# First feed-forward: the operand's low halves ahead of the second weight unit's remainder, and the first activation table loaded at the start

## The chip, the cores and the metric

The kernel runs on one core of one Trainium2 chip. The metric is the device time of one execution in microseconds (us); less is better. For the kernel before there are three timed runs, and one execution taken by the hardware profiler.

## The reference

Two transformer blocks, one behind the other, on 512 tokens of width 1024, all in float32. Only the first step of the first block matters here:

```python
def rms_norm(x, g):
    xf = x.astype(jnp.float32)
    y = xf * lax.rsqrt(jnp.mean(xf * xf, axis=-1, keepdims=True) + EPS)
    return (y * g.astype(jnp.float32)).astype(x.dtype)

def swiglu(h, w_gate, w_up, w_down):
    return (jax.nn.silu(h @ w_gate) * (h @ w_up)) @ w_down

x = x + 0.5 * swiglu(rms_norm(x, g_ffn1), w1_gate, w1_up, w1_down)   # D_FF = 2816
...
```

Behind it come a mixer with sparse and stick-breaking attention, a second feed-forward, a second mixer (mLSTM and differential attention) and a mixture of experts.

## The kernel before

**Products in three parts.** Each float32 product is made of three matmuls on a faster type. An operand is split into a high half (a rounded copy, made by ScalarE) and a low half (what the rounding left out, made by VectorE by subtraction). `mm3` (line 1178) issues high x high, high x low and low x high, for every k of the eight slices of the width. A slice is 128 x 512.

**The operand.** x lies transposed in `xT`, eight slices of 128 x 512. `operand` on ScalarE (line 1674) writes the high half `hH` of slice k, times the gain g_ffn1; `operand` on VectorE (line 2152) writes the low half `hL`. The factor of the norm is applied later: `square` on ScalarE (line 1678) squares a slice, `square` on VectorE (line 2156) adds it to `acc`, one matmul with a matrix of ones sums over the partitions, and `norm` on ScalarE (line 1664) takes the logarithm and the exponential of it. The products with w1_gate and w1_up are multiplied by that factor once they are done.

**Weight units.** Weights come in units of 128 x 1024 (512 KB), here the 128 columns of one output tile for all eight k. A ring of five landing tiles (`stage`) takes the transfers, and a ring of four (`wH`) the high halves. `round_weights` on ScalarE (line 1646) makes the high half of a unit, `remainder` on VectorE (line 2126) the low half, in place of the landed data. Unit 0 is the first tile of w1_gate, unit 1 the first of w1_up, unit 2 the second of w1_gate, and so on in turn. `weights_to(n)` on either engine handles all units up to n that have not been handled. In the steady state the engines handle unit i + 2 when TensorE is about to begin unit i (`AHEAD` is 2).

**Order.** Every engine has its own program and works it off in order; semaphores tie the programs together. TensorE's `dense` (line 1198) waits for the remainder of its unit (`w_lo`), and in the first unit also, ahead of each k, for the low half of the operand (`h`). So TensorE needs from VectorE: remainder 0 and low half 0, then low halves 1 to 7 one by one, then remainder 1, then the complete sum of squares for the norm's matmul, then remainder 2. The opening of the ScalarE program is at lines 2103 to 2111, that of the VectorE program at lines 2744 to 2751. VectorE's order is low half 0, remainder 0, low halves 1 and 2, remainder 1, low halves 3 to 7, squares. ScalarE's is high half 0, unit 0, high halves 1 to 7, squares 0 and 1, unit 1, squares 2 to 7.

**Transfers.** SyncE's program (line 2854 on) issues the gains (`cols`), then x in four pieces of two slices, with unit 0 behind the first piece, then unit 1, the constant matrices, units 2 and 3, more matrices, and from then on one unit whenever a landing tile is free.

**Activation tables.** ScalarE holds one set of functions at a time. `table(name)` (line 1637) remembers the set last asked for and issues a load when another is wanted; Copy and Square are in every set used here. Where an activation comes ahead of any load, the build puts one in front of it by itself. `norm` asks for "log_exp", the step `gate_r` behind it for "silu".

Of the kernel before, what the change touches and what calls it, by code (L numbers as in the profile page):

```python
# [20 lines left out]
NSTAGE, NSPLIT, AHEAD = 5, 4, 2  # L21
# [110 lines left out]
class Counts:  # L132
# [24 lines left out]
    def after(self, stream, *key):  # L157
        if not self.real:
            return None, 1
        name, n = self.at[(stream,) + key]  # L160
        return self.sem(name), n
# [73 lines left out]
def build(nc, A, out):  # L235
    with contextlib.ExitStack() as ctx:
# [1397 lines left out]
        def act_program(act):  # L1634
# [11 lines left out]
            def round_weights(u):  # L1646
                act.wait_ge(*after("land%d" % u.raw.at, u.i))
                free(u.high)
                act.activation(u.high.t[:, 0:u.size], u.raw.t[0][:, 0:u.size], ACT.Copy).then_inc(*did("w_hi", u.i))

            def weights_to(n):
                while state["unit"] <= min(n, M3.main - 1):
                    if not units[state["unit"]].whole:
                        round_weights(units[state["unit"]])
                    state["unit"] += 1
# [18 lines left out]
            def operand(s):  # L1674
                act.wait_ge(*after(*s.ready))
                act.activation(h[0][:, s.k, :], xT[:, s.k, :], ACT.Copy, scale=col(s.gain, s.k)).then_inc(*did("hh", s.gain, s.k))

            def square(s):
                act.wait_ge(*after(*s.ready))
                if s.k == 0:  # L1680
                    act.activation(acc[:, :], xT[:, 0, :], ACT.Square).then_inc(*did("acc0", s.gain))
                else:
                    if s.k > 2:
                        act.wait_ge(*after("acc", s.gain, s.k - 2))
                    act.activation(xsq[s.k % 2][:, :], xT[:, s.k, :], ACT.Square).then_inc(*did("sq", s.gain, s.k))
# [368 lines left out]
            def moe_stage(steps, M):  # L2054
# [35 lines left out]
                def region(x):  # L2090
                    seen = dict(act.passed)
                    state["table"] = None
                    counts.engine = "scalar_done_extra"
                    with act.when(count, x):
                        expert_steps(M.regions[x])
                        if x == 0:
                            for more in range(1, NX):
                                region(more)
                    act.passed, counts.engine = seen, "scalar_done"

                region(0)

            act.wait_ge(*after("cols_in",))
            for k in range(8):
                operand(Step("operand", gain="g_ffn1", k=k, ready=("x_in%d" % (k // 2),)))
                if k == 0:
                    weights_to(0)
            for k in range(8):
                square(Step("square", gain="g_ffn1", k=k, ready=("x_in%d" % (k // 2),)))
                if k == 1:  # L2110
                    weights_to(AHEAD - 1)
            ffn_stage(ffn1)
            mixer1_stage(mix1, M1)
            ffn_stage(ffn2)
# [4 lines left out]
        def dve_program(dve):  # L2119
# [6 lines left out]
            def remainder(u):  # L2126
                dve.wait_ge(*after("w_hi", u.i))
                dve.tensor_tensor(u.raw.t[1][:, 0:u.size], u.raw.t[0][:, 0:u.size], u.high.t[:, 0:u.size].bitcast(F32), ALU.subtract).then_inc(*did("w_lo", u.i))

            def weights_to(n):  # L2130
                while state["unit"] <= min(n, M3.main - 1):
                    if not units[state["unit"]].whole:
                        remainder(units[state["unit"]])
                    state["unit"] += 1
# [17 lines left out]
            def operand(s):  # L2152
                dve.wait_ge(*after("hh", s.gain, s.k))
                dve.scalar_tensor_tensor(h[1][:, s.k, :], xT[:, s.k, :], col(s.gain, s.k), h[0][:, s.k, :].bitcast(F32), ALU.mult, ALU.subtract).then_inc(*did("h", s.gain, s.k))
# [589 lines left out]
            for k in range(8):  # L2744
                operand(Step("operand", gain="g_ffn1", k=k))
                if k == 0:
                    weights_to(0)
                if k == 2:
                    weights_to(AHEAD - 1)
            for k in range(8):  # L2750
                square(Step("square", gain="g_ffn1", k=k))
            ffn_stage(ffn1)
# [160 lines left out]
        for program, done in ((sp_program, "sync_done"), (pe_program, "matmul_done"), (act_program, "scalar_done"),  # L2913
                              (dve_program, "vector_done"), (pool_program, "gpsimd_done")):
            run(program, Lane(None), done)
        counts.real = True
        counts.n = {}
        with nc.Block() as block:
            @block.sync
            def _(e):  # L2920
                run(sp_program, Lane(e), "sync_done")

            @block.tensor
            def _(e):
                run(pe_program, Lane(e), "matmul_done")

            @block.scalar
            def _(e):
                run(act_program, Lane(e), "scalar_done")

            @block.vector
            def _(e):
                run(dve_program, Lane(e), "vector_done")

            @block.gpsimd
            def _(e):
                run(pool_program, Lane(e), "gpsimd_done")
# [57 lines left out]
```

## Time and profile before

| | us |
|---|---|
| median of three runs | 2161.86 |
| the three runs | 2161.70, 2161.86, 2169.89 |
| time of the profiled execution | 2164.77 |
| its span | 2163.0 |
| TensorE busy (matmul) | 2065.1 (95% of the span) |
| VectorE busy | 1356.5 (63%) |
| ScalarE busy | 1019.1 (47%) |
| mean granted TensorE clock | 0.965 of full |

Times in the trace are counted from the start of the span; the execution's own time is 1.8 us longer than its span. Matmul ends are modelled, so the distance between starts is the safer measure of pace.

### The profile page before, as it was taken

To read this page: it belongs to the slowest core of one execution; us is meant where nothing else is said; L and a number is where in the kernel's file an instruction comes from. 1 tells how busy PE (TensorE), PEld (TensorE's weight loads), DVE (VectorE), ACT (ScalarE), POOL (GpSimd) and SP (SyncE) were. 2 spreads that over 40 slices of the span, in tenths; PEclk is the share of its full clock that TensorE was granted. 3 is DMA by queue.
4 is the path that set the end of the run, shared out by engine and by line. 5 is a ranking of instruction groups with operands and counts; after the bars stand their busy time and mean duration, and the time that the engine had idled before them with its cause. 6 is when DMAs were issued, how large, how long until landed. Compare 5 with 4: busy or idle time off the path is not lost.

```text
span 2163.0 us, 23488 instructions
## 1 busy us (share of the span) xinstructions
PE 2065.1 (95%) x9192; PEld 1575.6 (73%) x9192; DVE 1356.5 (63%) x1900; ACT 1019.1 (47%) x1504; POOL 125.7 (6%) x115
## 2 busy tenths in 40 slices
PE   7999999979999889999999999998979999999998
PEld 6888887746787668888888787775766666666664
DVE  5443544466666876544344465556788888888886
ACT  5222323344444354422122344555567777667773
POOL 0000000000000000000000000000012112111110
PEclk9999999988898899999999999999989999999999
DMA  5433334336334214333333332220549999999996
GB/s 179 146 99 110 90 96 80 85 48 65 55 61 67 73 40 146 96 96 91 101 96 97 88 101 58 56 59 25 184 173 397 394 391 392 391 386 384 390 386 231
DMA packets 289719, 351.68 MB, mean 163 GB/s; under 512 B 14768, under 2 KB 228784, under 8 KB 289600
## 3 DMA queue, kind: packets, MB, share of 16 engines
q1 hardware_dynamic: 280080, 326.43, 47.4%
q0 software_dynamic: 9520, 23.66, 3.1%
q8 instruction: 75, 1.23, 0.2%
q14 instruction: 44, 0.36, 0.0%
HBM read 337.71 MB, written 20.45 MB: 166 GB/s over the span
## 4 chain that ended last, share of the span: by engine, by line
PE 82%; DVE 10%; ACT 5%; DMA 1%; issue 1%; SPq 0%; DVEq 0%; ACTq 0%
PE bank L181 81%; PE bank L184 2%; ACT p L187 1%; DMA stage<-w_in 1%; ACT wH L187 1%; DVE PTL L193 1%; DVE y L193 1%; DVE score L217 1%; ACT T L187 1%; ACT rr L187 1%; DVE st L205 1%; DVE p L196 1%; DVE top L214 1%; DVE stage2L L193 0%; DVE gt L193 0%
## 5 line engine op out<-in xcount | busy, mean ns | idle before, releaser
L181 PE MATMUL bank<-hH,wH 128*128 128x512 f32 x1104 | 445.8, 404 | 14.4 <-DVE stage0L L193 9.9
L181 PE MATMUL bank<-hL,wH 128*128 128x512 f32 x1104 | 438.1, 397 | 0.0
L187 ACT ACTIVATE wH<-stage 128x1024 fp32r<-128x1024 f32 (+3 forms) x265 | 262.4, 1002 | 98.8 <-PE bank L181 81.4
L181 PEld LDWEIGHTS bank<-hH,wH 128*128 128x128 f32 x1104 | 213.7, 194 | 65.8 <-DVE stage0L L193 9.9
L181 PEld LDWEIGHTS bank<-hL,wH 128*128 128x128 f32 x1104 | 213.6, 193 | 45.1 <-issue 1.2
L187 ACT ACTIVATE w_moe<-stage_moe 128x1024 fp32r<-128x1024 f32 x158 | 156.8, 1047 | 0.2 <-issue 0.2
L181 PE MATMUL bank<-w_moe,xS 128*128 128x512 f32 x382 | 154.0, 403 | 0.0
L181 PE MATMUL bank<-hidH,wH 128*128 128x512 f32 x352 | 137.4, 390 | 2.1 <-DVE stage2L L193 0.9
L181 PE MATMUL bank<-hidL,wH 128*128 128x512 f32 x352 | 136.9, 389 | 0.0
L187 ACT ACTIVATE hidH<-hf 128x512 fp32r<-128x512 f32 x44 | 27.8, 632 | 189.1 <-DVE hf L193 189.1
L199 DVE SCALAR_TENSOR_TENSOR xT<-bank,xT 128x512 f32<-128x512 f32 x32 | 22.1, 692 | 133.6 <-PE bank L181 133.6
L187 ACT ACTIVATE sg<-sg 128x512 f32<-128x512 f32 x60 | 36.9, 628 | 124.5 <-DVE sg L193 124.5
L181 PEld LDWEIGHTS bank<-w_moe,xS 128*128 128x128 f32 x382 | 71.8, 188 | 30.9 <-issue 16.2
L193 DVE TENSOR_TENSOR stage1L<-stage,wH 128x1024 fp32r<-128x1024 f32 (+2 forms) x56 | 67.1, 1199 | 40.1 <-ACT wH L187 39.8
L181 PE MATMUL bank<-hH,stage3L 128*128 128x512 f32 x232 | 91.7, 395 | 0.0
L181 PE MATMUL bank<-hH,stage1L 128*128 128x512 f32 x224 | 88.4, 395 | 0.0
L181 PE MATMUL bank<-stage_moe,hF 128*64 128x512 f32 x192 | 87.5, 598 | 0.0
L181 PE MATMUL bank<-hH,stage2L 128*128 128x512 f32 x216 | 86.0, 398 | 0.0
L181 PE MATMUL bank<-hH,stage4L 128*128 128x512 f32 x216 | 85.5, 396 | 0.0
L193 DVE TENSOR_TENSOR stage0L<-stage,wH 128x1024 fp32r<-128x1024 f32 (+3 forms) x56 | 63.7, 1137 | 34.2 <-ACT wH L187 33.7
L187 ACT ACTIVATE hH<-xT,cols 128x512 fp32r<-128x512 f32 x40 | 28.3, 721 | 119.7 <-DVE xT L199 83.8
L181 PE MATMUL bank<-hH,stage0L 128*128 128x512 f32 x208 | 83.1, 400 | 0.0
(576 smaller groups left out, 4565.9 us busy)
## 6 DMA issues: line engine op xcount, KB each, us to landing
stage<-w_up SPq DMA_DIRECT2D x88, 512.0 KB, 5.8
stage_moe<-w_gate SPq DMA_DIRECT2D x88, 512.0 KB, 6.3
stage_moe<-w_down SPq DMA_DIRECT2D x88, 512.0 KB, 7.4
stage<-w_gate SPq DMA_DIRECT2D x84, 512.0 KB, 5.5
stage_moe<-w_up SPq DMA_DIRECT2D x84, 512.0 KB, 7.8
stage<-w_in SPq DMA_DIRECT2D x58, 512.0 KB, 4.4
stage<-w_down SPq DMA_DIRECT2D x56, 512.0 KB, 6.7
pair_results<-zero POOLq DMA_DIRECT2D x8, 512.0 KB, 2.9
```

What stands on the lines that cost most here:

```text
L181: return self.e.matmul(*a, **k) if self.e is not None else Nothing()
L184: return self.e.transpose(*a, **k) if self.e is not None else Nothing()
L187: return self.e.activation(*a, **k) if self.e is not None else Nothing()
L193: return self.e.tensor_tensor(*a, **k) if self.e is not None else Nothing()
L196: return self.e.tensor_scalar(*a, **k) if self.e is not None else Nothing()
L199: return self.e.scalar_tensor_tensor(*a, **k) if self.e is not None else Nothing()
L205: return self.e.tensor_reduce(*a, **k) if self.e is not None else Nothing()
L214: return self.e.max(*a, **k) if self.e is not None else Nothing()
L217: return self.e.match_replace(*a, **k) if self.e is not None else Nothing()
```

## The change

The ScalarE program asks for the silu set ahead of its first wait. Both programs then work through all eight slices of the operand before they turn to unit 1 (`AHEAD - 1` is 1), and take the squares behind that. TensorE's, GpSimd's and SyncE's programs are as they were.

```diff
@@ -2100,15 +2100,15 @@
 
                 region(0)
 
+            table("silu")
             act.wait_ge(*after("cols_in",))
             for k in range(8):
                 operand(Step("operand", gain="g_ffn1", k=k, ready=("x_in%d" % (k // 2),)))
                 if k == 0:
                     weights_to(0)
+            weights_to(AHEAD - 1)
             for k in range(8):
                 square(Step("square", gain="g_ffn1", k=k, ready=("x_in%d" % (k // 2),)))
-                if k == 1:
-                    weights_to(AHEAD - 1)
             ffn_stage(ffn1)
             mixer1_stage(mix1, M1)
             ffn_stage(ffn2)
@@ -2745,8 +2745,7 @@
                 operand(Step("operand", gain="g_ffn1", k=k))
                 if k == 0:
                     weights_to(0)
-                if k == 2:
-                    weights_to(AHEAD - 1)
+            weights_to(AHEAD - 1)
             for k in range(8):
                 square(Step("square", gain="g_ffn1", k=k))
             ffn_stage(ffn1)
```

## Rows read from the trace of the kernel before

**Rows 1.** The page, part 4: shares of the chain that ended last, by engine.

```profile
PE 82%; DVE 10%; ACT 5%; DMA 1%; issue 1%; SPq 0%; DVEq 0%; ACTq 0%
```

**Rows 2.** That chain in order of time, 0 to 80 us: start, duration, what.

```profile
5.61 1.28 ACT L187
...
16.82 63.21 PE bank L181 x269
```

**Rows 3.** Timeline, TensorE, 9 to 30 us: start, duration, instruction [idle before, releaser].

```profile
9.89 0.80 PE L181 MATMUL bank<-hH,wH 128*128 128x512 f32 x1 [9.89 <-DVE stage0L L193]
10.48 0.63 PE L181 MATMUL bank<-hL,wH 128*128 128x512 f32 x1
...
13.04 0.45 PE L181 MATMUL bank<-hL,wH 128*128 128x512 f32 x1
13.33 0.40 PE L181 MATMUL bank<-hH,stage0L 128*128 128x512 f32 x1
16.82 0.79 PE L181 MATMUL bank<-hH,wH 128*128 128x512 f32 x1 [3.10 <-DVE hL L199]
...
21.84 0.40 PE L181 MATMUL bank<-hH,wH 128*128 128x512 f32 x1
...
27.29 1.02 PE L181 MATMUL bank<-acc,mats 128*128 128x512 f32 x2
27.75 0.79 PE L181 MATMUL bank<-hH,wH 128*128 128x512 f32 x1
```

**Rows 4.** Timeline, ScalarE (two rows), then VectorE, 0 to 40 us.

```profile
8.48 4.38 ACT L187 ACTIVATE hH<-xT,cols 128x512 fp32r<-128x512 f32 x7
...
23.78 1.99 ACT L187 ACTIVATE wH<-stage 128x1024 fp32r<-128x1024 f32 x2
...
7.66 0.75 DVE L199 SCALAR_TENSOR_TENSOR hL<-xT,cols,hH 128x512 fp32r<-128x512 f32 x1 [7.66 <-ACT hH L187]
...
9.75 1.41 DVE L199 SCALAR_TENSOR_TENSOR hL<-xT,cols,hH 128x512 fp32r<-128x512 f32 x2
14.88 1.23 DVE L193 TENSOR_TENSOR stage1L<-stage,wH 128x1024 fp32r<-128x1024 f32 x1 [3.73 <-ACT wH L187]
16.02 3.40 DVE L199 SCALAR_TENSOR_TENSOR hL<-xT,cols,hH 128x512 fp32r<-128x512 f32 x5
19.34 5.47 DVE L193 TENSOR_TENSOR acc<-acc,xsq 128x512 f32<-128x512 f32 x7
```

**Rows 5.** Four issues of SyncE; under each its KB and us from issue to landing.

```profile
1.67 0.43 SPq L223 DMA_DIRECT2D stage<-w_gate  x1
stage<-w_gate SPq DMA_DIRECT2D x1, 512.0 KB, 5.5
...
3.24 0.52 SPq L223 DMA_DIRECT2D xT<-x  x1
xT<-x SPq DMA_DIRECT2D x1, 512.0 KB, 7.9
...
3.80 0.45 SPq L223 DMA_DIRECT2D stage<-w_up  x1
stage<-w_up SPq DMA_DIRECT2D x1, 512.0 KB, 9.1
...
7.37 3.89 SPq L223 DMA_DIRECT2D stage<-w_up  x1
stage<-w_up SPq DMA_DIRECT2D x1, 512.0 KB, 10.0
```

**Rows 6.** Busy time by stretch, single engines, then granted clock, DMA share, GB/s.

```profile
16.60:20.00 3.40, 3.17 (x8) 2.50 (x9) 3.40 (x6) 0.00 (x0) 0.00 (x0) 0.50 0.82 239
400.00:760.00 360.00, 326.24 (x1470) 254.52 (x1470) 235.43 (x448) 159.93 (x280) 8.67 (x16) 0.88 0.38 64
```

**Rows 7.** Groups of instructions, the table loads: count, busy, mean ns, idle before.

```profile
L190 ACT ACT_TABLE_LOAD x14 | 18.0, 1283 | 27.7 <-PE bank L181 19.4 <-DVE so L193 5.6 <-DVE sg L193 1.6
L187 ACT ACT_TABLE_LOAD x1 | 1.3, 1283 | 5.6 <-DMA xT<-x 5.6
```

## Prediction

> **What bounds the kernel now.** I read the chain that ended last first, as shares and then in order of time over the first 80 us; then the TensorE timeline of the opening, then ScalarE and VectorE beside it, then the landing times of the first transfers. The chain is 82% TensorE [rows 1], and from 16.82 us on it is TensorE without a gap for far longer than the 80 us asked for [rows 2]. So the body of the kernel is a line of matmuls, and time taken out ahead of 16.82 us moves everything behind it. Before that the chain holds a table load of 1.28 us at 5.61 [rows 2], ScalarE's high halves and the remainder of the second weight unit at 14.88 [rows 4].
>
> The TensorE timeline shows what that costs. The first matmul starts at 9.89, behind the remainder of unit 0. Nine matmuls (three of the eight k) run, and then the engine stands for 3.10 us until 16.82, waiting for a VectorE low half [rows 3]. The cause is in the order of VectorE's work. Low halves 1 and 2 are done at 11.16; then VectorE sits 3.73 us idle for the rounded high half of unit 1, makes its remainder from 14.88, and only at 16.02 begins low halves 3 to 7, which TensorE needs first [rows 4]. ScalarE had all eight high halves ready at 12.86 (8.48 + 4.38) [rows 4]. The stall is a matter of order, not of capacity.
>
> It costs a second time. At the start matmuls 2 to 8 are 0.427 apart ((13.04 - 10.48)/6), and the step from 8 to 9 is 0.29: the pace has just risen. In unit 1 it is 0.227 ((27.29 - 21.84)/24). But behind the stall the other fifteen matmuls of unit 0 take 5.02, from 16.82 to 21.84, where 15 x 0.227 would be 3.41 [rows 3]: the granted clock is at 0.50 from 16.6 to 20.0, the lower level of 1.2 GHz [rows 6].
>
> **The change, part by part.** I rebuild the opening with the durations and start-to-start distances of the rows.
>
> *The table load.* Before, it runs at 5.61, behind the wait for x, and the first high half, at 6.9, follows its end (5.61 + 1.28) [rows 2]. After, it is issued ahead of every wait, with some 4.8 us of idle ScalarE as its cover (0.8 to 5.6) against its 1.28. No other load is added: the trace has fourteen loads by the helper and one automatic one [rows 7], and Copy and Square both run while the silu set is in, so the automatic one should go. If the cover were gone, the cost would be what it is today. The first high half then starts at about 5.6 and ends near 6.3. But next on ScalarE is the rounding of unit 0, and that transfer was issued at 1.67 and landed 5.5 later, at 7.17 [rows 5]. So rounding starts at about 7.24 and not at 7.54 (where it would follow today's high half): of 1.28 us only 0.30 arrives. The rest is idle ScalarE waiting for weights. First matmul: 9.89 - 0.30 = 9.59. Bounds: 0 (if the landing slips by 0.3) and 1.28 (if it came early).
>
> *The order on VectorE.* With the start 0.30 earlier, low half 1 begins at 9.45. The five in a row take (3.40 - 0.75)/4 = 0.66 each, start to start, where 0.75 is one alone [rows 4], so low half 7 begins at 9.45 + 6 x 0.66 = 13.4 and is done at 14.2. ScalarE supplies ahead of it: seven high halves take 4.38 from about 8.18, so to 12.56; the last pair of x lands at 3.24 + 7.9 = 11.1 [rows 5], before high half 6 would start (11.25). That margin is 0.1 us, and even if it is lost VectorE does not want high half 6 until 12.7.
>
> *TensorE.* Matmul 1 at 9.59, matmul 2 0.59 later [rows 3], then 0.427 each while the clock is low. In the profiled execution the pace changed at about 13.2, between matmuls 8 and 9. If it does so at the same time, matmul 9 starts near 13.17, matmul 10 near 13.45, and the remaining ones follow at 0.227: matmul 24 at 13.45 + 14 x 0.227 = 16.63, and unit 1 at 16.86. k = 3 is wanted at 13.4 and has been there since 11.5; k = 7 is wanted at about 16.0 and is there at 14.2. No low half is late.
>
> *What is late next: the remainder of unit 1.* Its weights were issued at 3.80 and landed 9.1 later, at 12.90 [rows 5]. ScalarE, free at 12.56, rounds them from 12.97 to 14.01; VectorE takes the remainder at 14.1, done at 15.3. TensorE wants it at 16.86: 1.6 us to spare. So the wait that is moved behind the low halves does not hold TensorE. Queued behind it on VectorE are only the sums of squares.
>
> *Sums of squares, and units 2 and 3.* Rounding unit 1 now comes ahead of the squares on ScalarE, but VectorE's seven additions set the pace. They start right after the remainder, at 15.23 and not 19.34, and take 5.47 [rows 4]: done at 20.7. TensorE reaches the norm matmul after 24 matmuls, which took 27.29 - 21.84 = 5.45 before, hence at 22.31; unit 2 begins 0.46 behind that, as before at 27.75 [rows 3]. Spare: 1.6. The remainder of unit 2 follows from 20.75 to 21.98, wanted at 22.77: spare 0.8, the smallest margin in the new opening. Both roundings before it start at 19.7 instead of 23.78 [rows 4]; the data of unit 3, issued at 7.37, is there at 17.4 [rows 5]. The transfers that follow wait for TensorE's completions and move with it.
>
> *Sum.* Unit 1 starts at 16.86 instead of 21.84 [rows 3]: 4.98, call it 5.0. It has three parts: 3.26 is the stall (13.33 to 16.82, less one 0.23); 1.61 is the second slow stretch (5.02 against 3.41); 0.30 is the table, of which about half is lost again, since the start falls in the slow pace. Everything later waits on something earlier, not on a fixed time, so the shift is carried to the end. Span 2163.0 - 5.0 = 2158.0; the profiled execution's own time 2164.8 - 5.0 = 2159.8. The median of the three runs was 2161.9, 2.9 below that execution, so my figure for the median is 2161.9 - 5.0 = **2156.9**.
>
> **The rivals.**
>
> *A: the low clock lasts longer in the new opening (12%).* What speaks for it: no row says what would fix the moment of the rise, and in this trace the low stretch behind the stall lasted 3.4 us [rows 6]. If the slow pace lasted that much longer in the new opening, 8 matmuls would run in place of 15, and 7 x 0.227 = 1.6 us go. The gain is 3.4: median 2158.5. Against: the engine is busier than before from its first matmul on. On the pages: the Trainium skill ("TensorE: Matmul & The Clock Gate", Part 1: The HAM clock gate) says that the gate's count runs free of the kernel, so that the moment of the rise varies from run to run; the trace has one execution only and can neither bear that out nor refute it.
>
> *B: the table's full 1.28 us arrives (4%).* That needs the first weights about 1 us earlier than in the trace. Nothing in the change moves a transfer. It would add 0.5 (in the slow pace half of an earlier start is lost) to 1.0: gain about 5.7, median 2156.2.
>
> *C: the gain is absorbed or the table part is void (8%).* Should the automatic load stay, 0.30 is lost: 2157.2. Should unit 2's remainder come more than 0.8 us late (ScalarE and VectorE alternate on squares in steps of 0.8, so one lost step uses the margin), TensorE pauses at 22.8 and perhaps 1 to 3 us return: 2158 to 2160.
>
> *D: the clock of the first mixer (6% to the slow side of before, 4% to the fast side).* From 400 to 760 us the granted clock averages 0.88 [rows 6], so (1 - 0.88) x 2 x 360 = 86 us lie at the low level. A matmul costs 0.427 there against 0.227, so a further 3.4 us at that level costs up to 3.4 x 0.47 = 1.6. The new opening shifts the mixer against whatever sets these stretches. From four more low stretches on the gain is gone (4 x 1.6 = 6.4: median 2163); for 0.5% slower it takes ten more. For it: the three runs of the same kernel spread by 8 us. Against: it can as well go the other way (the 4%, which adds 6 us or more to the gain), and most such stretches come from the stage's own waits, which the change does not touch.
>
> **How the numbers follow.** Forecast 66% (2156.9, give or take 1.5), A 12%, B 4%, C 8%, D 6% slow and 4% fast. The range takes in A to C (2156 to 2160) and the spread that the runs of one kernel show, in either direction: D's first step above, the same mechanism in our favour below. 2151 to 2164. A measurement of this kernel tells a change from none at about 0.5%, which is 10.8 us. The forecast and A, B and C lie within it. Only D reaches beyond: all its 4% on the fast side, where the gain of 5.0 adds to it, and 2 of its 6% on the slow side.
>
> **What would show it.** The first ScalarE row is a load by the helper's line, before 3 us. High half 0 starts at 5.6, the rounding of unit 0 at 7.2, now with an idle that a transfer ends. First matmul at 9.6. VectorE: seven low halves in a row from about 9.45, remainder of unit 1 at 14.1. TensorE: no idle between matmul 9 and 10, unit 1 from 16.9, norm matmul near 22.3. Table switch behind the norm at 23.3, not 28.3. I would be wrong if TensorE shows a new wait at 16.9 (unit 1's remainder) or at 22.8 (unit 2's), if the clock falls inside the opening all the same, or if the shift of 5.0 at 28 us has shrunk by the end of the feed-forward.

## The result and the profile after

| | before | after |
|---|---|---|
| median, us | 2167.01 (22 runs, 2161.48 to 2170.30) | 2161.68 (22 runs, 2155.32 to 2165.81) |
| time of the profiled execution | 2164.77 | 2162.40 |
| its span | 2163.0 | 2160.6 |
| first matmul of unit 0 / of unit 1 / norm matmul, at us | 9.89 / 21.84 / 27.29 | 9.47 / 17.48 / 22.92 |

The change is faster: ratio 0.9978, 95% interval 0.9971 to 0.9985, which is 5.3 us between the medians. The kernel before was run again beside it, and its median over 22 runs is 2167.01. The three runs shown earlier had given 2161.86, close to the lowest of the 22. Beside the experiments below the same kernel gave medians of 2165.21, 2165.19 and 2166.04 (33, 33 and 23 runs).

The TensorE timeline of the changed kernel, to be laid beside [rows 3]; columns are start, duration, instruction, and in brackets the idle before it:

```profile
9.47 0.79 PE L181 MATMUL bank<-hH,wH 128*128 128x512 f32 x1 [9.47 <-DVE stage0L L193]
10.06 0.63 PE L181 MATMUL bank<-hL,wH 128*128 128x512 f32 x1
...
13.05 0.63 PE L181 MATMUL bank<-hH,stage0L 128*128 128x512 f32 x1
13.47 0.63 PE L181 MATMUL bank<-hH,wH 128*128 128x512 f32 x1
...
14.33 0.60 PE L181 MATMUL bank<-hH,stage0L 128*128 128x512 f32 x1
14.76 0.40 PE L181 MATMUL bank<-hH,wH 128*128 128x512 f32 x1
14.99 0.39 PE L181 MATMUL bank<-hL,wH 128*128 128x512 f32 x1
...
17.48 0.39 PE L181 MATMUL bank<-hH,wH 128*128 128x512 f32 x1
...
22.92 1.02 PE L181 MATMUL bank<-acc,mats 128*128 128x512 f32 x2
23.38 0.79 PE L181 MATMUL bank<-hH,wH 128*128 128x512 f32 x1
```

Only the first row has an idle. k = 3 follows k = 2 at once (13.47 behind 13.05), where [rows 3] has 3.10 us. But the slow pace, 0.43 from start to start, lasts twelve matmuls, up to 14.76, and not the eight of [rows 3].

ScalarE (first six rows) and VectorE in the same execution, beside [rows 4]:

```profile
0.75 1.28 ACT L190 ACT_TABLE_LOAD   x1 [0.75 <-PEq L2987]
5.43 0.72 ACT L187 ACTIVATE hH<-xT,cols 128x512 fp32r<-128x512 f32 x1 [3.40 <-DMA xT<-x]
7.10 1.06 ACT L187 ACTIVATE wH<-stage 128x1024 fp32r<-128x1024 f32 x1 [0.95 <-DMA stage<-w_gate]
8.06 4.38 ACT L187 ACTIVATE hH<-xT,cols 128x512 fp32r<-128x512 f32 x7
12.77 1.06 ACT L187 ACTIVATE wH<-stage 128x1024 fp32r<-128x1024 f32 x1 [0.33 <-DMA stage<-w_up]
...
23.97 1.28 ACT L190 ACT_TABLE_LOAD   x1 [2.42 <-PE bank L181]
...
9.33 4.72 DVE L199 SCALAR_TENSOR_TENSOR hL<-xT,cols,hH 128x512 fp32r<-128x512 f32 x7
13.97 1.22 DVE L193 TENSOR_TENSOR stage1L<-stage,wH 128x1024 fp32r<-128x1024 f32 x1
15.10 5.47 DVE L193 TENSOR_TENSOR acc<-acc,xsq 128x512 f32<-128x512 f32 x7
20.63 1.23 DVE L193 TENSOR_TENSOR stage2L<-stage,wH 128x1024 fp32r<-128x1024 f32 x1
```

The load is over at 2.03, and the next row is 3.40 us of waiting for x. The one behind it shows why the load's 1.28 us don't arrive: ScalarE then stands 0.95 us for the transfer of w_gate. VectorE works without a gap from 9.33 on, and unit 1's remainder is done at 15.19, 2.3 us before TensorE begins unit 1.

The chain that ended last, in order of time (start, duration, what), says the same in one view, beside [rows 2]. The table and all of the operand's high halves have left it, and a weight transfer stands in their place:

```profile
1.67 5.41 DMA stage<-w_gate
7.08 0.02 issue
7.10 1.06 ACT wH L187
8.16 0.02 issue
8.19 1.24 DVE stage0L L193
9.43 0.04 issue
9.47 70.73 PE bank L181 x298
```

The groups of table loads, beside [rows 7]: fifteen by the helper, and no automatic one is left.

```profile
L190 ACT ACT_TABLE_LOAD x15 | 19.2, 1283 | 28.2 <-PE bank L181 19.2 <-DVE so L193 5.6 <-DVE sg L193 1.6
```

### The profile page after: what moved, and what is told of

Read it like the earlier page. It is cut to its first block, busy times and chain, and to the rows that moved or that the text cites. A ratio compares the mean times of both kernels' runs of the same rounds, so it can differ in the third digit from the quotient of the medians.

```text
span 2160.6 us, 23488 instructions
## 1 busy us (share of the span) xinstructions
PE 2067.6 (96%) x9192; PEld 1576.3 (73%) x9192; DVE 1356.9 (63%) x1900; ACT 1019.5 (47%) x1504; POOL 126.7 (6%) x115
## 4 chain that ended last, share of the span: by engine, by line
PE 83%; DVE 10%; ACT 5%; DMA 1%; issue 1%; SPq 0%; DVEq 0%; ACTq 0%
PE bank L181 81%; PE bank L184 2%; ACT p L187 1%; DMA stage<-w_in 1%; DVE PTL L193 1%; ACT wH L187 1%; DVE y L193 1%; DVE score L217 1%; ACT T L187 1%; ACT rr L187 1%; DVE st L205 1%; DVE p L196 1%; DVE top L214 1%; DVE stage2L L193 0%; DVE gt L193 0%
```

## The experiments

Ratios are to the kernel before, run on the same chip in the same turns, with 95% intervals. "Unit 1" is the start of its first matmul in the profiled execution; "pace rises" is the first matmul that starts less than 0.3 us behind the one before it.

| kernel | ratio | first matmul | pace rises | unit 1 |
|---|---|---|---|---|
| before | 1 | 9.89 | 13.33 (and again 20.2) | 21.84 |
| the change | 0.9978 (0.9971 to 0.9985) | 9.47 | 14.99 | 17.48 |
| order only | 0.9980 (0.9971 to 0.9989) | 9.78 | 15.34 | 17.88 |
| table only | 1.0004 (0.9995 to 1.0014) | 9.55 | 21.74 | 22.43 |
| VectorE's order only | 0.9981 (0.9972 to 0.9991) | 10.23 | 13.59 | 17.23 |
| ScalarE's order only | 0.9993 (0.9983 to 1.0002) | 9.71 | 16.44 | 19.42 |
| stall filled | 0.9993 (0.9982 to 1.0004) | 9.82 | in the extra matmuls | 20.32 |
| nine warm-up matmuls | 0.9974 (0.9965 to 0.9984) | 11.70 | ahead of unit 0 | 17.56 |
| first piece of x halved | 0.9978 (0.9969 to 0.9987) | 8.48 | 13.6 | 16.32 |
| both of these | 0.9980 (0.9970 to 0.9989) | 11.48 | ahead of unit 0 | 17.35 |
| four warm-up matmuls | 0.9970 (0.9959 to 0.9981) | 9.60 | ahead of unit 0 | 15.37 |
| the change again | 0.9983 (0.9972 to 0.9994) | 9.62 | 14.60 | 17.35 |

### The change in parts

Order only is the change without its `table("silu")`:

```diff
-            table("silu")
             act.wait_ge(*after("cols_in",))
```

> The new order on ScalarE and VectorE, the table load left as before (automatic, behind the wait for x). Order theory (the stall came from VectorE's order, the table brings 0.3 to 0.4): first matmul at 9.9 as before, no idle behind matmul 9, unit 1 from 17.2 to 18 according to when the pace rises, ratio 0.998 (4.0 to 4.9 us). Rival (the table is worth its full 1.28, the order the rest): gain 3.0 to 3.6, unit 1 not before 18.5.

Ratio 0.9980, first matmul 9.78, no idle behind it, unit 1 at 17.88. That is 3.96 us earlier than before, with a late rise of the pace (15.34). The order carries the gain.

Table only is the kernel before with that line added.

> Only the table load moved to the start. Order theory: every ScalarE row of the opening that waits for nothing newer moves by 0.3 to 0.45, because unit 0's landing at 7.1 ends the wait: first matmul 9.5, stall still 3.1, its end at 16.4 to 16.5; a gain of 0.4, which the times can't tell from none. Rival (the full 1.28 arrives): first matmul 8.6, stall ends at 15.5.

First matmul 9.55, stall until 16.61 (2.85 long), and no gain in time (1.0004). Unit 1 even begins 0.6 us later than before (22.43), because here the slow pace behind the stall lasts until 21.74. The rows of ScalarE:

```profile
0.75 1.28 ACT L190 ACT_TABLE_LOAD   x1 [0.75 <-PEq L2989]
5.53 0.72 ACT L187 ACTIVATE hH<-xT,cols 128x512 fp32r<-128x512 f32 x1 [3.50 <-DMA xT<-x]
7.18 1.06 ACT L187 ACTIVATE wH<-stage 128x1024 fp32r<-128x1024 f32 x1 [0.93 <-DMA stage<-w_gate]
```

1.28 us are taken out and 0.93 come back as a wait for w_gate. What is left, 0.3 to 0.4 us, is less than the times can tell. The full-1.28 rival is out: it wanted the first matmul at 8.6.

VectorE's order only keeps ScalarE's old order. Its edit is this one in VectorE's program; ScalarE's order only, further down, is the change's moved line in ScalarE's program and nothing else:

```diff
             for k in range(8):
                 operand(Step("operand", gain="g_ffn1", k=k))
                 if k == 0:
                     weights_to(0)
-                if k == 2:
-                    weights_to(AHEAD - 1)
+            weights_to(AHEAD - 1)
```

> Only VectorE's order changed; ScalarE still rounds unit 1 behind squares 0 and 1, at 13.8 to 14.9, and the table is as before. Order theory: low half 7 is done at 14.5, the remainder of unit 1 runs 14.9 to 16.1, TensorE wants it at 17.2 or later, so the whole order gain is there: 4.0 to 4.9 us, no idle on TensorE. Rival (both moves are needed): TensorE waits at the start of unit 1 for the remainder, and the gain stays under 3.

One edit of VectorE's program gives all of it: ratio 0.9981, unit 1 at 17.23, no idle on TensorE. That unit 1 comes earlier here than with order only (17.88) is no merit of the order: neither has an idle behind the first matmul, and the pace rose at 13.59 here and at 15.34 there. VectorE waits 0.42 us for ScalarE's rounding ahead of the remainder:

```profile
10.10 4.72 DVE L199 SCALAR_TENSOR_TENSOR hL<-xT,cols,hH 128x512 fp32r<-128x512 f32 x7
15.24 1.23 DVE L193 TENSOR_TENSOR stage1L<-stage,wH 128x1024 fp32r<-128x1024 f32 x1 [0.42 <-ACT wH L187]
```

The remainder is done at 16.47, and TensorE wants it at 17.23. So moving unit 1's rounding ahead of the squares on ScalarE bought nothing that can be seen.

> Only ScalarE's order changed: unit 1 is rounded right behind the high halves, VectorE keeps its order and waits for it after low half 2. Order theory: rounding from 12.97 (unit 1 lands at 12.9), remainder from 14.0, low half 3 at 15.9, so the stall shrinks from 3.1 to about 2.2: gain 0.9. Rival (the cause was ScalarE's late rounding, for which VectorE stood 3.73 us): gain of 3 us or more and a stall under 1.

As the order theory had it: VectorE's wait shrinks from 3.73 to 2.95, k = 3 starts at 15.87 and not 16.82, ratio 0.9993. TensorE's rows:

```profile
15.87 0.51 PE L181 MATMUL bank<-hH,wH 128*128 128x512 f32 x1 [1.95 <-DVE hL L199]
```

Unit 1, though, comes 2.42 us earlier than before, not 0.9: here the fifteen matmuls behind the stall take 3.55 us (15.87 to 19.42), against 5.02 in [rows 3]. The other 1.5 us is pace: here it was already high when the stall ended, with nothing put into the stall. The next experiment looks at that.

### The pace behind the stall

Eight extra matmuls in the kernel before, where TensorE would stand. They read data already used and write a bank that nobody reads; their result is dropped.

```diff
                     if s.ready == "norm":
+                        if s.gain == "g_ffn1" and k == 3:
+                            for _ in range(8):
+                                pe.matmul(banks.t[0][:, :], u.H[:, 0, :], s.act[0][:, 0, :], start=True, stop=True)
                         pe.wait_ge(*after("h", s.gain, k))
```

> The kernel before, with eight extra matmuls on unit 0's first slice into an unused bank between k = 2 and k = 3, where TensorE would stand; their result is not used. The stall's end stays where it was, since VectorE ends it. Clock theory (about 1.6 of the gain comes from the pace that falls again behind the stall): k = 3 starts at 16.5 to 16.9 as before, the matmuls behind it go 0.23 apart in most executions, unit 1 starts at 20.3 instead of 21.8, gain 1 to 1.6 us. Rival (the slow pace there is not the stall's doing, or extra matmuls hold up k = 3): no gain, or 0.5 to 1.5 slower.

```profile
13.83 2.67 PE L181 MATMUL bank<-hH,wH 128*128 128x512 f32 x8
16.75 0.50 PE L181 MATMUL bank<-hH,wH 128*128 128x512 f32 x1 [0.25 <-DVE hL L199]
17.09 0.40 PE L181 MATMUL bank<-hL,wH 128*128 128x512 f32 x1
17.32 0.40 PE L181 MATMUL bank<-hH,stage0L 128*128 128x512 f32 x1
```

k = 3 starts at 16.75, as before. Behind it the matmuls go 0.23 apart and unit 1 starts at 20.32 instead of 21.84: 1.52 us, of which 1.45 is pace (the fifteen matmuls take 3.57 and not 5.02). In the stretch from 16.6 to 20.0 (columns as in [rows 6]) fourteen matmuls are counted where before had eight, and the granted clock reads 1.00, where it was 0.50. The count is the evidence: a reading of 1.00 can also stand over the slow pace, as the last section shows.

```profile
16.60:20.00 3.40, 3.25 (x14) 2.63 (x15) 3.35 (x6) 0.01 (x1) 0.00 (x0) 1.00 0.81 238
```

The ratio, 0.9993 (0.9982 to 1.0004), has its middle where 1.5 us belongs, and doesn't exclude zero. So the rival's second half is out: the extra matmuls did not hold up k = 3. That they brought the pace is not shown as firmly. It is one execution, and of the three with the stall left open two went on slow (before, until 20.2; table only, until 21.7) and one, with a stall of 1.95, at the full pace (ScalarE's order only). Repeated profiles of before and of this kernel would have to tell; there are none.

### What the opening still loses

After the change the opening's remaining loss is the slow pace of the first twelve matmuls. Two edits go at that, both on top of the change.

```diff
+            pe.wait_ge(*after("zero",))
+            for _ in range(9):
+                pe.matmul(banks.t[0][:, :], zero[:, 0:128], zero[:, 0:512], start=True, stop=True)
             ffn_stage(ffn1)
```

> The changed kernel, with nine extra matmuls on a tile of zeros into an unused bank ahead of unit 0, from 1.8 us on; their result is not used. Clock theory (what the opening still loses is the slow pace from 9.5 to 13 or 15): if activity on zeros counts, unit 0 runs at 0.23 from the start and takes 5.5 us, so its end is at 15.0; then the remainder of unit 1, done at 15.2, ends the wait: unit 1 at 15.3 to 15.4 instead of 17.5, gain 1.5 to 2 us over the changed kernel. Rival (the pace is set by a fixed time from the start of the program, or zeros don't count): unit 1 at 17 to 17.8, no gain.

Half right. Matmuls on zeros do bring the pace up, and unit 0 runs at 0.23 from its third matmul on (5.9 us for its 24). But the nine held TensorE until 11.7, each of them 1.71 us at the slow pace and 0.86 at the fast one, so unit 0 began 2.2 us late, and unit 1 at 17.56 instead of 15.3. Gain and loss cancel.

The other edit splits x's first transfer, so that less lies ahead of unit 0:

```diff
-            for k in range(4):
-                sp.dma_start(xT[:, 2 * k:2 * k + 2, :], ...)
-                if k == 0:
-                    load(units[0])
+            sp.dma_start(xT[:, 0:1, :], ...)
+            load(units[0])
+            sp.dma_start(xT[:, 1:2, :], ...)
+            for k in range(1, 4):
+                sp.dma_start(xT[:, 2 * k:2 * k + 2, :], ...)
```

> The changed kernel, with x's first transfer (two slices) split: slice 0, then unit 0, then slice 1. Landing theory (the table's 1.28 arrives only in part because unit 0 lands at 7.1): 256 KB less are ahead of unit 0, at some 390 GB/s 0.67 us; unit 0 lands at 6.4 to 6.5, first matmul at 8.8 to 8.9 instead of 9.5, and since the pace is slow there about half of 0.65 reaches unit 1: 0.3 to 0.65. Rival (landing is bound by latency, not by what is ahead): first matmul stays at 9.4 to 9.5.

(ScalarE's first high half now waits for slice 0 alone.) The first piece lands 0.9 us earlier, unit 0 1.0 us earlier, and the first matmul is at 8.48, a little more than expected:

```profile
4.57 0.72 ACT L187 ACTIVATE hH<-xT,cols 128x512 fp32r<-128x512 f32 x1 [2.54 <-DMA xT<-x]
6.11 1.06 ACT L187 ACTIVATE wH<-stage 128x1024 fp32r<-128x1024 f32 x1 [0.81 <-DMA stage<-w_gate]
...
13.64 1.06 ACT L187 ACTIVATE wH<-stage 128x1024 fp32r<-128x1024 f32 x1 [0.38 <-DMA stage<-w_up]
```

The last row is the price: unit 1's weights arrive 0.9 later than with the change (12.77), so that its remainder is done at 15.97, 0.35 us before it is wanted. Unit 1 starts at 16.32, 1.16 us ahead of the change. About 0.5 of that is the earlier start at the slow pace, the rest an earlier rise of the pace. In the times it is one with the change (0.9978).

> Both of the two edits before this on the changed kernel. If both theories hold: first matmul at 8.8, pace 0.23, low half 7 at 13.4, but unit 1's weights land at 12.8 all the same, its remainder is done at 15.1 to 15.2, and unit 1 starts at 15.3: with TensorE waiting about 0.9 there, no more than the warm start alone. Rival (what ends last is the low halves, 0.66 apart): unit 1 moves by a further 0.6.

Inconclusive: with nine warm-up matmuls the first matmul is at 11.48 whatever lands earlier, so what it was to tell apart didn't come into play.

Four warm-up matmuls instead of nine (the same diff with `range(4)`), with the change as it is beside it on the same chip:

> The changed kernel with four extra matmuls on zeros from 1.8 us on, not nine: with nine they ran until 12.1 and held unit 0 up by 2.5 us. At 0.855 per half matmul while the pace is low and 0.43 after, four are done between 7.8 and 8.6, ahead of 9.5. Clock theory: unit 0 runs 9.5 to 15.0 at 0.23, unit 1 starts at 15.2 to 15.4, held by its own remainder; norm matmul at 20.8. Gain over the changed kernel 1.5 to 2.5 us. Rival (the idle of 1 to 1.7 us before unit 0 lets the pace fall again): unit 0 slow, unit 1 at 17 or later, no gain.

> The changed kernel as it is, beside the four extra matmuls on the same chip. Opening as in its first profile but for the moment at which the pace rises, which moved between 13.1 and 15.2 in the profiles so far: unit 1 from 16.9 to 17.9. Ratio to before 0.9975 to 0.998. Rival (the moment of the rise is a property of the kernel): unit 1 at 17.5 again, to 0.1.

```profile
1.76 5.66 PE L181 MATMUL bank<-zero 128*128 128x512 f32 x8 [1.76 <-POOL zero L220]
9.60 0.50 PE L181 MATMUL bank<-hH,wH 128*128 128x512 f32 x1 [2.18 <-DVE stage0L L193]
...
14.99 0.39 PE L181 MATMUL bank<-hH,stage0L 128*128 128x512 f32 x1
15.37 0.50 PE L181 MATMUL bank<-hH,wH 128*128 128x512 f32 x1
```

All as the clock theory had it: the pace holds through 2.18 us of idle, unit 0 takes 5.4 us and is issued by 15.0, unit 1 starts at 15.37, where its remainder, done at 15.32, lets it. The norm matmul is at 20.98, against 22.79 in the change's second profile. Medians 2159.49 and 2160.81, ratios 0.9970 and 0.9983. Their intervals overlap, so of a version better than the change one execution of each shows 1.8 us in the opening, and the times only agree in sign.

The change's second profile, with unit 1 at 17.35 and the rise at 14.60, doesn't decide its own question: 0.13 from the first is neither clearly the same nor clearly other. In the two executions of this one kernel the first fast matmul comes 5.52 and 4.98 us behind the first matmul. Across all kernels it comes 3.4 to 5.6 us behind wherever no idle lies between (13.59 behind 10.23, 15.34 behind 9.78), with the same work of TensorE in front of it. So the moment moves between executions. This agrees with what the Trainium skill says, as cited in the prediction ("TensorE: Matmul & The Clock Gate", Part 1: The HAM clock gate), that the moment of the rise varies from run to run. The reason it gives, a count that runs free of the kernel, no run here shows.

## Why the prediction was right or wrong

**The level was wrong, and with it the absolute time.** 2156.9 was forecast and 2161.68 measured, although the difference, 5.0 forecast and 5.3 measured, agrees. The term that failed is the median of three, 2161.86. Over 22 runs the median of before is 2167.01. Two of the three runs were at the low end (all later medians of this kernel lie between 2165.2 and 2167.0), and the third, 2169.89, which I took for spread, was nearer to the middle than the other two. The profiled execution (2164.77) was the better anchor; I had noted that it stood 2.9 above and went by the lower number. The time lay in the range because that had been widened by the spread of the three; 2161.68 is what that level would have given with no gain at all. That forecast and measured difference are only 0.3 apart is partly luck: the opening gave 4.4, not 5.0, and the interval of the measured difference reaches from 3.3 to 6.3.

**The step that failed: from a gain of 5.0 us to a change that can't be told from none.** The prediction put the bound of what a measurement can tell at 0.5%, 10.8 us. No row gives that figure; the only spread at hand was that of three single runs, 8 us. My chances put 94% on "within the bound". The change is smaller than 0.5% (0.22%), but it can be told from none: 22 runs on either side give an interval of plus or minus 0.07%, about 1.5 us, and the gain of 5.3 us is clear of none by three times that. My own sum gave a gain in each of the cases A to C. A forecast that is certain of its sign should say so in words, however small its size.

**The stall: right, in place, cause and size.** 3.26 forecast; k = 3 now follows at once. VectorE's order was the cause and not ScalarE's lateness: VectorE's order only has the whole gain, ScalarE's order only a stall of 1.95.

**The second slow stretch: right in one execution, and not constant.** 1.61 forecast; filling the stall gave 1.52 at unit 1, 1.45 of it in the pace. But with only the table moved, the fifteen matmuls behind the stall took 5.82 (16.61 to 22.43), with only ScalarE's order 3.55 (against 3.41 at full pace). The term lies between 0.1 and 2.4 by the moment of the rise. One profile had given me one value for it.

**The table: right in mechanism, small in size either way.** 0.30 forecast at the first matmul, 0.42 in the change's profile, 0.34 with the table alone, mixed up with what x's landing moves from one execution to the next (the wait for it ended at 5.43 to 5.96 in these profiles). Counted from the end of that wait, the first matmul comes 4.27 or 4.28 later in the five profiles without the early load, and 3.98 to 4.10 later in four with it (the change twice, table only, four warm-up matmuls). So the early load is worth 0.2 to 0.3 us there. The wait for w_gate that takes its place was named, with its place (7.24 forecast, 7.10 found).

**The first slow stretch: too short.** I let the pace rise at 13.2, as in the trace of before; it rose at 14.8, and four more matmuls went at 0.43 for 0.8 us. That is rival A, at half its size. Gain at unit 1: 4.36, not 4.98.

**The margins held.** Unit 1's remainder was done at 15.19 (15.3 forecast), the sum of squares at 20.6 (20.7), unit 2's remainder at 21.86 (21.98), and TensorE reached them at 17.48, 22.92 and 23.38. The last margin was 1.5 instead of 0.8, because TensorE was later than forecast. Rival C did not come. With the late pieces of x in the second profile of the change (ScalarE waited until 12.09 for the last) unit 1's remainder began at 14.95, a full us later than in the first, and TensorE did not wait.

**"The shift is carried to the end": right as a mean, wrong for two single profiles.** The same ScalarE instructions in both kernels, before first, then after (one in the first feed-forward, one in the first mixer, one in the mixture of experts just behind the second mixer, one near the end):

```profile
42.23 0.63 ACT L187 ACTIVATE hidH<-hf 128x512 fp32r<-128x512 f32 x1 [2.69 <-DVE hf L193]
455.26 0.63 ACT L187 ACTIVATE qiH<-y 128x512 fp32r<-128x512 f32 x1 [6.27 <-DVE y L193]
1611.30 0.60 ACT L187 ACTIVATE gS<-bank 128x512 f32<-128x512 f32 x1 [7.18 <-PE bank L181]
2150.49 0.59 ACT L187 ACTIVATE yo<-bank 64x512 f32<-64x512 f32 x1 [7.54 <-PE bank L181]
```

```profile
37.87 0.63 ACT L187 ACTIVATE hidH<-hf 128x512 fp32r<-128x512 f32 x1 [2.69 <-DVE hf L193]
449.83 0.63 ACT L187 ACTIVATE qiH<-y 128x512 fp32r<-128x512 f32 x1 [4.98 <-DVE y L193]
1607.43 0.60 ACT L187 ACTIVATE gS<-bank 128x512 f32<-128x512 f32 x1 [5.94 <-PE bank L181]
2147.56 0.59 ACT L187 ACTIVATE yo<-bank 64x512 f32<-64x512 f32 x1 [8.52 <-PE bank L181]
```

The shift is 4.36 at the start, 5.43 in the first mixer, 3.87 behind the second mixer and 2.93 near the end, and the spans differ by 2.4. In the second profile of the change the same last instruction is at 2143.68: there the shift grew from 4.50 to 6.81. With the filled stall it grew from 1.53 to 5.77, more than that edit can have done; from 400 to 760 us the granted clock was 0.91 there, 0.89 with the change and 0.88 before. So later stages add or take some 2 us, in one case 4, from one execution to another. Rival D named where (the mixers, by the granted clock); the runs bear it out as far as they go: over the 22 runs of the change the time falls as the mean granted clock rises (correlation -0.87, about 1 us for each 0.001), from 2165.81 us at 0.963 to 2155.32 us at 0.970. What moves the clock there was not isolated by an experiment and stays open. What is shown is that two single spans can't measure an edit of this size; the opening's own rows and medians over many runs can, and they agree: 4.4 to 4.5 us and 5.3 (3.3 to 6.3 by the interval).

## What to carry to other kernels

Where a consumer takes items one by one and one big item is needed only later, put the small ones first on the producer's queue. Here one moved line on VectorE did it, and the matching move on the engine before it and the table load added nothing that the times can see. A stall of TensorE can be charged twice, once for its length and once for the slow pace behind it, so price both, and the second as a range (here 0.1 to 2.4 us). When a hidden cost is removed at the start of a kernel, look for the transfer that lands next; and for a gain of some us in two thousand, fix the baseline with tens of runs before giving a number.

## What the runs showed of the hardware

- The granted clock reads 1.00 at the very start of every trace (9 to 12 us), although in those without warm-up matmuls the first ones start 0.427 us apart. With only the table moved the pace did not rise until 21.7, and still the same stretch reads 1.00 (third number from the end), with 8 matmuls in it, where the change has 17. So a 1.00 at the start does not show that the pace is high, and the distance of starts is what to read there.

```profile
16.60:20.00 3.40, 3.39 (x8) 2.71 (x9) 3.29 (x6) 0.16 (x1) 0.00 (x0) 1.00 0.83 242
```

- Behind 2.18 us of idle TensorE went on at the full pace (four warm-up matmuls), behind 3.10 (before) and 2.85 (table only) at the slow one. Behind 1.95 (ScalarE's order only) it went on at the full pace although it had been at the slow one when the idle began. Each is one execution.
- The pace also rises during matmuls on a tile of zeros. Each leaves two records; these start 0.855 us apart at first and 0.43 from 6.95 on with nine of them, from 5.97 on with four.
- Four useless matmuls in otherwise idle time ahead of the first useful one moved unit 1 by 2.0 us (17.35 to 15.37, one execution of each).
